# Recurrent mixer of a fused transformer kernel: where the weight stream's steps stand between two chains

## The reference

```python
def step(state, inp):
    r_t, w_t, k_t, v_t, a_t, b_t = inp
    sa = jnp.einsum('bhvk,bhk->bhv', state, a_t)
    state = (state * w_t[:, :, None, :] + sa[..., None] * b_t[:, :, None, :]
             + v_t[..., None] * k_t[:, :, None, :])
    return state, jnp.einsum('bhvk,bhk->bhv', state, r_t)
...
u = x @ w_in[l]
y_rwkv = _rwkv7_branch(rcols, rg, ...)       # the step above over 256 tokens, 8 heads of 64
mix = jnp.concatenate([y_conv, y_mla, y_rwkv], axis=-1)
x = _layer_norm(DEEPNORM_ALPHA * x + mix @ w_out[l], ln_g[l], ln_b[l])
```

## Time and profile before

| what | value |
|---|---|
| median of three runs | 2423.23 us |
| profiled execution, span of the instructions | 2420.8 us |
| TensorE busy | 2346.3 us, 97% |
| weight loads into TensorE busy | 2025.2 us, 84% |
| VectorE busy | 1465.8 us, 61% |
| ScalarE busy | 1129.3 us, 47% |
| GpSimd busy | 196.8 us, 8% |
| granted TensorE clock, mean | 0.994 |
| bytes moved | 415.77 MB, 172 GB/s |

### The profile page before, as it was taken

How to read it: one execution, slowest core, us unless ns; L and a number is a source line. 1 busy time by engine, 2 the same in 40 slices (tenths; PEclk the granted TensorE clock), 3 DMA queues, 4 the chain that set the end, 5 groups by cost and what they waited for, 6 DMA issues and landing times.

```text
span 2420.8 us, 38838 instructions
## 1 busy us (share of the span) xinstructions
PE 2346.3 (97%) x16401; PEld 2025.2 (84%) x16401; DVE 1465.8 (61%) x1852; ACT 1129.3 (47%) x1566; POOL 196.8 (8%) x200
## 2 busy tenths in 40 slices
PE   7999999999999999999999999999999999999997
PEld 7777777888888888888888899889898899899985
DVE  4899966766554554454444445745755568456556
ACT  5565556644544444444444434433554535334542
POOL 4000000002000000000000001220000051301000
PEclk9999999999999999999999999999999999999998
DMA  9544454455566666666555576434547574335465
GB/s 245 157 157 148 155 193 149 163 193 182 183 191 186 188 191 184 191 191 191 189 191 189 190 222 177 118 98 116 165 132 244 168 216 141 98 106 156 139 208 168
DMA packets 260366, 415.77 MB, mean 172 GB/s; under 512 B 53448, under 2 KB 74440, under 8 KB 259424
## 3 DMA queue, kind: packets, MB, share of 16 engines
q1 hardware_dynamic: 254496, 395.63, 53.1%
q0 software_dynamic: 5376, 17.56, 2.5%
q10 hardware_dynamic: 320, 0.08, 0.0%
HBM read 406.90 MB, written 7.87 MB: 171 GB/s over the span
## 4 chain that ended last, share of the span: by engine, by line
PE 82%; DVE 12%; ACT 3%; issue 2%; DMA 1%; ACTq 0%; SPq 0%; DVEq 0%
PE banks L585 80%; DVE wp_hl L1166 4%; ACT wp_hl L1861 2%; DVE u_z L1497 1%; DVE nsd L1560 1%; DVE u_z L1479 0%; PE banks L697 0%; ACT L1861 0%; DMA raw<-w_in 0%; DVE r_SA L1701 0%; PE banks L709 0%; PE banks L822 0%; DMA xt<-x 0%; DVE xt L1478 0%; DVE r_SA L1667 0%
## 5 line engine op out<-in xcount | busy, mean ns | idle before, releaser
L1166 DVE TENSOR_TENSOR wp_hl<-raw,wp_hl 128x1024 fp32r<-128x1024 f32 x740 | 915.4, 1243 | 862.8 <-ACT wp_hl L1861 861.9
L1861 ACT ACTIVATE wp_hl<-raw 128x1024 fp32r<-128x1024 f32 x740 | 783.1, 1060 | 1087.3 <-PE banks L585 1054.5
L585 PE MATMUL banks<-wp_hl,XX_hl 128*128 128x512 f32 x3840 | 899.7, 393 | 10.5 <-DVE wp_hl L1166 10.5
L585 PEld LDWEIGHTS banks<-wp_hl,XX_hl 128*128 128x128 f32 x3840 | 715.8, 188 | 174.7 <-DVE wp_hl L1166 16.9
L585 PE MATMUL banks<-XX_hl,wp_hl 128*128 128x256 f32 x4992 | 646.2, 287 | 9.7 <-DVE wp_hl L1166 7.5
L585 PEld LDWEIGHTS banks<-XX_hl,wp_hl 128*128 128x128 f32 x4992 | 611.3, 192 | 28.0 <-issue 14.1
L585 PE MATMUL banks<-wp_hl,FF_hl 128*128 128x512 f32 x1056 | 240.7, 389 | 0.0
L585 PEld LDWEIGHTS banks<-wp_hl,FF_hl 128*128 128x128 f32 x1056 | 197.9, 188 | 41.0
L585 PE MATMUL banks<-wp_hl,MM_hl 128*128 128x512 f32 x384 | 88.4, 390 | 0.0
L585 PE MATMUL banks<-wp_hl,MXa_hl 128*128 128x512 f32 x384 | 88.3, 389 | 0.0
L585 PEld LDWEIGHTS banks<-wp_hl,MXa_hl 128*128 128x128 f32 x384 | 72.1, 188 | 14.9
(11 more groups left out here) (439 smaller groups left out, 1771.2 us busy)
## 6 DMA issues: line engine op xcount, KB each, us to landing
raw<-w_in SPq DMA_DIRECT2D x304, 512.0 KB, 3.9
raw<-w_out SPq DMA_DIRECT2D x96, 512.0 KB, 4.4
raw<-w_ffn_gate SPq DMA_DIRECT2D x88, 512.0 KB, 3.5
raw<-w_ffn_up SPq DMA_DIRECT2D x88, 512.0 KB, 3.5
raw<-w_ffn_down SPq DMA_DIRECT2D x88, 512.0 KB, 3.5
raw<-w_proj_attn SPq DMA_DIRECT2D x16, 512.0 KB, 4.2
raw<-w_proj_ssm SPq DMA_DIRECT2D x16, 512.0 KB, 3.6
raw<-w_glu SPq DMA_DIRECT2D x8, 512.0 KB, 3.6
```

Of the source, the lines that this page charges most:

```text
L585: return e.matmul(o, lhsT, rhs, start=start, stop=stop, skip_group_check=True)
L1166: return tt(d, src, hi, SUB)
L1861: return e.activation(o, x, func, bias=bias, scale=scale)
```

## The change

`rwkv_turns` keeps the order of the stages. Behind chain 0's stage it now yields a share of 0 and carries that share over to chain 1's stage of the same round, behind which both shares come together. Only in round 0, where chain 1 has no stage yet, does chain 0's share stand behind its own stage. All four engines use the same generator, so both stages of a round follow each other directly on each of them. All later lines stand four lines further down.

```diff
--- before.py
+++ after.py
@@ -121,10 +121,14 @@
 
 def rwkv_turns():
 
-    for i in range(len(RWKV_SHARES) + 1):
+    n, due = len(RWKV_SHARES), 0
+    for i in range(n + 1):
         for c in range(2):
-            if 0 <= i - c < len(RWKV_SHARES):
-                yield c, i - c, RWKV_SHARES[i - c]
+            if 0 <= i - c < n:
+                due += RWKV_SHARES[i - c]
+                last = c == 1 or i == 0
+                yield c, i - c, due if last else 0
+                due = 0 if last else due
 
 
 def v3(a, n):
```

## The result

| | before | after |
|---|---|---|
| median of 4 runs each, same chip | 2421.82 us | 2438.46 us |
| lowest and highest | 2419.87, 2423.90 | 2435.26, 2439.90 |
| span of the profiled execution | 2420.8 us | 2438.1 us |
| granted TensorE clock, mean | 0.994 | 0.990 |
| mixer of layer 0, from its first matmuls (wa, w2a) to the sums of squares (sqr, cst) | 180.57 us | 189.31 us |

A forecast was written before the change was run, and what follows sets the result against it. TensorE, busy 97%, was taken as the bound, by its work and its standstills. Per layer 9.3 us of losses less 3.1 gave +6.2; two layers +12.4, plus 2.4 from span to median and 0.8 for the clock: 2436.4 us, range 2428 to 2445.

The forecast's parts named there:

- Part 1, handovers: Whole mixer: 17 fewer runs of steps on TensorE at 0.18 us each, a gain of 3.1 us per layer.
- Rival C: Handovers between steps and mixer matmuls cost more, 0.55 us or above each, so the kernel gets faster; chance 0.08.
- Part 2, the first pause: Chain 0's stage 2, chain 1's stage 1: TensorE waits 4.2 us for VectorE's split instead of 1.3, +2.9 per layer.
- Part 3, the second pause: One round later, chain 0's stage 3, chain 1's stage 2 on VectorE: TensorE pauses 2.7 us, +2.3 per layer.
- Part 4: Doubling levels: four 0.47 us stalls stay; chain 1's sum costs nothing except at the last level, +0.5 us per layer.
- Part 5, r_rv: Mixer's end: r_rv wait grows from 0.5 to 2.5 us, +2.0; new wait for GpSimd's square, +1.6, per layer.
- The clock: Half clock behind the first pause might cost 1.5 us per layer, in neither or one; 0.8 us counted in all.
- B: Both first pauses bring half clock, outlasting the second pause: 1.5 to 3.9 us per layer, 2439 to 2443; chance 0.25.
- A: Terms as summed, the clock falls at most once: 2436.4 us, own range 2432 to 2440; chance 0.45.
- Rival D: Handovers give 0.28 us each and the second pause doesn't come: +3.6 us, 2426.8; chance 0.10.
- Rival E: VectorE's stage 2 products, beside GpSimd's, draw each other out further, so pauses are larger: 2441 to 2448; chance 0.12.

The follow-up runs named there:

- experiment 3: Kernel before, with both chains' stages together only in rounds 4 to 9, 18, 19, 20 and 23: 2419.64 against 2422.35 us, -2.7 us.
- experiment 10: Kernel before, with shares of stages 5 and 18 at 1.5 and 0.75 and rounds 1, 6 to 9, 19, 20, 23, 24 merged: 2412.08 against 2421.80 us.
- experiment 9: Changed kernel with rounds 2 and 3 in the old order on TensorE alone: 2442.16 us against 2421.42 for the kernel before, +20.7 us.
- experiment 4: Changed kernel with round 27 alone as before: 2430.41 us against 2422.35 for the kernel before, +8.1 us.
- experiment 5: Changed kernel with round 2 alone as before: 2434.89 us against 2421.42 for the kernel before, +13.5 us.
- experiment 2: Kernel before, with both chains' stages together only in rounds 24 to 27: 2432.16 against 2422.35 us, +9.8 us.
- experiment 8: Changed kernel with rounds 2 and 3 in the old order on ScalarE and VectorE alone: 2435.08 us against 2421.42 for the kernel before, +13.7 us.
- experiment 1: Kernel before, with both chains' stages together only in rounds 1, 2 and 3: 2431.74 against 2422.35 us, +9.4 us.

## Why the prediction came out

The forecast was 2436.4 us and the run gave 2438.46; as a change, +13.2 was forecast and +16.6 measured. The pauses came where they were forecast; their sizes were partly off, and the clock was far off. The 2 us hide one missed term and two that were too large.

- **Part 1, handovers: right.** 0.18 us each was taken. The account above leaves 0.15 to 0.16, experiment 3 gives 0.19 to 0.21 and experiment 10 0.23 to 0.24. Rival C (0.55 or more) has fallen.
- **Part 2, the first pause: right.** 4.2 forecast, 4.07 measured in both layers, and experiment 9 shows that it comes with VectorE's order.
- **Part 3, the second pause: mis-sized.** 2.7 forecast, 1.50 measured. I let r_bon start when VectorE had done its splits, 2.4 us after the late split. But it waits for TensorE's stage 3 and started 4.2 us after it (1531.54 against 1527.35). From there the block with the split took 10.3 us, not 11.4: two of its products took 0.82 and 0.68 us, where I had counted the 1.8 us they take beside GpSimd, and the wait for ScalarE was 0.9 instead of 1.2; against that, the r_t products at its end took 1.90 us instead of 0.87. TensorE came 2.0 us later than forecast, 1.8 of it from the low clock. In sum 4.2 + 10.3 - 13.0 = 1.5. The late r_bon and the late TensorE are mostly the same low clock and cancel; what is left of the miss is the block's 1.1 us.
- **Part 4: right.** The four stalls stayed at 0.47, and the fifth, forecast at 0.5, is 0.46.
- **Part 5, r_rv: too large.** 2.5 forecast, 1.73 measured. The lost cover of 0.8 was there. ScalarE's squares delayed the rounding by 0.4 us instead of 0.7, and the 0.5 us for "shorter steps in between" doesn't exist. GpSimd's wait was right, 1.49 for 1.6.
- **The clock: the failed step.** "I count 0.8 us in all." It was 4.9 and 4.2 us, 9.1 in all. One half of that is the half clock behind the first pause, in both layers (1.8 and 2.6 us), where the forecast had one fall at most. The prediction had expected that half clock until 9 us after the pause would cost up to 4 us, and that the pause of part 3 would swallow most of it. The clock was back after 4.0 and 5.3 us, and the pause swallowed none: r_bon and, over ScalarE's copy, the first product with r_y wait for TensorE's slow stage 3. So VectorE is late by the same amount: TensorE came 0.8 us later in the second layer, r_bon began 0.5 us later, the wait for ScalarE was 0.4 us longer, and the pause is 1.50 us in both. The other half (3.1 and 1.5 us) I did not foresee at all. I had listed the two pauses at the mixer's end, 2.5 and 1.6 us, and compared only the 4.2 us one with the earlier trace rows.

So of the cases it is B by its first condition, both first pauses bringing the clock down. B's second condition did not hold: the half speed ended before the pause of part 3. B's range of 2439 to 2443 begins 0.5 us above the median; the time fell into A's own range because the overcounted pauses (1.2 + 0.8 us per layer) made up for half of the clock, and because the median lies only 0.4 us above the profiled span here, where I had added 2.4. The 2.4 held no fixed cost of that size: each run's time is 1.8 us above its own span, and the rest is the difference between one execution and the median. The forecast's nearness is partly luck: on the span it was +13.2 against +17.3. Rival D has fallen, since the pause of part 3 came (1.50 us); no mixer gives 0.28 for a handover either, though the medians do not exclude it. Its sum was also off: it takes off 2.7 for that pause where the sum above holds 2.3, so it should have read 2427.6. Rival E has fallen, too: taken together, VectorE's products of that block took 1.0 us less in the new order, in both layers, not more.

The Trainium skill (TensorE: Matmul & The Clock Gate, "HAM oscillation — how this bites in real kernels") says that a long pause between bursts of matmuls sends the array back to half its clock, each time. This trace agrees at the 4.07 us pauses of both layers; it does not cover what experiments 4 and 5 show, below.

## What to carry to other kernels

Before two blocks of a helper engine are put back to back, compare their sum with the work that lies ready for the bottleneck engine; merge only where the buffers cover both, and look at the order of all engines: here neither VectorE's old order alone (+13.7 us) nor TensorE's (+20.7 us) undid the loss. Price a pause by its own length and by the slow matmuls that may follow, and add up pauses that stand close together. A delay is hidden by a later pause only if what ends that pause does not itself wait for the delayed engine.

## What the runs showed of the hardware

- Two pauses of TensorE of 1.73 and 1.49 us, with 1.0 us of matmuls between, were followed by half clock in after and in experiment 2; the first of them alone was not (experiment 4).
- The pair was followed by half clock each of the ten times that it stands in the traces (after and experiments 2, 5, 8 and 9, two layers each), and so was the pause of 4.05 to 4.08 us each of eight times (after and experiments 1, 4 and 9, two layers each).
- In between, a pause of 2.73 us was followed by full clock in one layer and by half clock in the other, in the same execution (experiment 5). With 2.76 us the clock fell in both layers (experiment 8), with 2.61 and 2.63 us in neither (experiment 9). What decides is open; I did not test it. After the 4.07 us pause the slow spell cost 1.8 us in one layer and 2.6 in the other.
- VectorE's product of two 128x512 tiles took 0.68 us at 1536.44 and 1.67 us at 1537.16, in the same block. GpSimd, after:

```profile
1536.46 1.83 POOL L2414 TENSOR_TENSOR r_SA<-r_kp,r_AQ 128x512 f32<-128x512 f32 x1 [0.49 <-ACT r_AQ L1865]
```

It runs from 1536.46 to 1538.29. VectorE's first product had begun just ahead of it. The second began within it, and ended 0.54 us after it. That fits one engine waiting for the other's whole instruction; no experiment took GpSimd's work away to test it. The Trainium skill (SBUF — State Buffer, "SBUF: two separate sides") describes such a lock, held by whichever starts first; this row agrees.
